# Attention stages in pairs of heads, value and output projection woven in

## The reference

```
stick:  z = q k^T * scale;  log_keep = past ? -softplus(z) : 0
        tail = reversed cumsum(log_keep) - log_keep
        w = past ? exp(log_sigmoid(z) + tail) : 0;   out = (w v) @ w_o
moba:   q, k turned by partial rotary; with 256 tokens there is one block,
        so causal softmax(q k^T * scale) v;           out = (...) @ w_o
mla:    q from a normed latent (head 64 + 32 rotary), k and v from another,
        causal softmax(...) v;                        out = (...) @ w_o
```

## Time and profile before

| | |
|---|---|
| median of 3 runs | 2904.25 us (2901.33 to 2906.99) |
| profiled execution | span 2897.5 us, 44300 instructions; the page gives no other time of it |
| PE busy | 2740.8 us (95%) |
| PE weight loads busy | 2491.1 us (86%) |
| DVE busy | 1697.9 us (59%) |
| ACT busy | 1285.5 us (44%) |
| DMA | 454.85 MB, 157 GB/s over the span |
| chain that ended last | PE 87%, DVE 6%, ACT 4%, issue 1%, DMA 1% |

### The profile page before, as it was taken

The page is one execution under the profiler, slowest core; times in us unless marked ns, Lnnn a source line. Parts: engine busy times, 40 slices in busy tenths (PEclk is TensorE's granted clock), DMA queues, the critical chain, the costliest instruction groups (busy, mean ns, idle before and its releaser), DMA issues.

```text
span 2897.5 us, 44300 instructions
## 1 busy us (share of the span) xinstructions
PE 2740.8 (95%) x18332; PEld 2491.1 (86%) x18342; DVE 1697.9 (59%) x1903; ACT 1285.5 (44%) x1376; POOL 6.8 (0%) x17
## 2 busy tenths in 40 slices
PE   7899998998999989999988999999799999998998
PEld 6689886997999869999976799999679999986997
DVE  6665576656555546565555455655655565564555
ACT  5443454334434544443433434444444444355433
POOL 0000000000000000000000000000000000000000
PEclk9899998999999999999998999999899999998999
DMA  7245432554454325545432255454315545541452
GB/s 270 87 177 189 174 139 82 194 191 148 162 189 165 139 84 184 194 174 187 179 139 80 101 189 189 175 188 170 115 45 201 179 171 201 184 153 70 163 185 73
DMA packets 63473, 454.85 MB, mean 157 GB/s; under 512 B 7104, under 2 KB 7360, under 8 KB 8848
## 3 DMA queue, kind: packets, MB, share of 16 engines
q1 hardware_dynamic: 61920, 448.82, 42.7%
q0 software_dynamic: 1024, 3.51, 0.3%
q10 hardware_dynamic: 432, 1.13, 0.1%
HBM read 452.38 MB, written 1.05 MB: 156 GB/s over the span
## 4 chain that ended last, share of the span: by engine, by line
PE 87%; DVE 6%; ACT 4%; issue 1%; DMA 1%; SPq 0%; DVEq 0%; ACTq 0%
PE tb L226 14%; PE tb L229 14%; PE tb L228 14%; PE acc L257 11%; PE acc L258 10%; PE acc L259 10%; DVE w_lo L206 2%; PE acc L226 1%; PE acc L228 1%; PE acc L229 1%; ACT w_hi L199 1%; PE tb L634 1%; PE tb L288 1%; PE acc L664 1%; PE tb L632 1%
## 5 line engine op out<-in xcount | busy, mean ns | idle before, releaser
L206 DVE TENSOR_TENSOR w_lo<-raw,w_hi 128x2048 fp32r<-128x2048 f32 x426 | 973.8, 2290 | 477.6 <-ACT w_hi L199 477.6
L199 ACT ACTIVATE w_hi<-raw 128x2048 fp32r<-128x2048 f32 x426 | 811.6, 1910 | 582.6 <-PE tb L229 302.9
L226 PE MATMUL tb<-xT,w_hi 128*128 128x256 f32 x3520 | 1004.0, 285 | 15.0 <-DVE w_lo L206 12.4
L228 PE MATMUL tb<-xT,w_hi 128*128 128x256 f32 x3520 | 997.4, 283 | 0.0
L229 PE MATMUL tb<-xT,w_lo 128*128 128x256 f32 x3520 | 997.2, 283 | 0.0
L226 PEld LDWEIGHTS tb<-xT,w_hi 128*128 128x128 f32 x3520 | 676.4, 192 | 24.4 <-DVE w_lo L206 8.1
L228 PEld LDWEIGHTS tb<-xT,w_hi 128*128 128x128 f32 x3520 | 676.6, 192 | 4.5
L229 PEld LDWEIGHTS tb<-xT,w_lo 128*128 128x128 f32 x3520 | 676.6, 192 | 0.0
L257 PE MATMUL acc<-w_hi,cat 128*128 128x512 f32 x1152 | 453.1, 393 | 10.1 <-DVE cat L674 6.5
L258 PE MATMUL acc<-w_hi,cat 128*128 128x512 f32 x1152 | 450.7, 391 | 0.0
L259 PE MATMUL acc<-w_lo,cat 128*128 128x512 f32 x1152 | 449.4, 390 | 0.0
(11 more groups left out here) (260 smaller groups left out, 2427.3 us busy)
## 6 DMA issues: line engine op xcount, KB each, us to landing
raw<-in_stream SPq DMA_DIRECT2D x426, 1024.0 KB, 4.8
h<-in_x SPq DMA_DIRECT2D x2, 512.0 KB, 4.9
gain<-in_gains POOLq DMA_DIRECT2D x2, 512.0 KB, 9.3
xn<-in_gates POOLq DMA_DIRECT2D x2, 512.0 KB, 8.4
out<-xn SPq DMA_DIRECT2D x2, 512.0 KB, 2.7
cst<-in_consts ACTq DMA_DIRECT2D x1, 960.5 KB, 12.5
big<-in_pT POOLq DMA_DIRECT2D x2, 256.0 KB, 3.0
gain<-in_gains POOLq DMA_DIRECT2D x1, 320.0 KB, 3.6
```

The costliest lines, as they stand in the source:

```text
L199: act.activation(w_hi[:, k % SPLIT, :], raw[:, k % RAW, :], ACT.Copy).then_inc(hi_done, 1)
L206: dve.tensor_tensor(w_lo[:, k % SPLIT, :], raw[:, k % RAW, :], w_hi[:, k % SPLIT, :], ALU.subtract).then_inc(lo_done, 1)
L226: pe.matmul(dst(f), hi, src[:, kt, 0, :], start=kt == 0 and (after is None or f == 0), stop=False, skip_group_check=after is not None)
L228: pe.matmul(dst(f), hi, src[:, kt, 1, :], start=False, stop=False, skip_group_check=after is not None)
```

## The change

- `plan` now lists the products of chunks 3 to 11, in the order query, key, value for each group of four heads; the stream is laid out in that order. `begin` makes only the first query, key and value chunk, with the spread of the norm's factor in the middle of the second.
- Value chunks are poured between heads too; ACT takes them (`v_take`).
- Heads go in pairs in moba and mla: the scores of both heads lie in banks 0 and 1 of `tb`, the transposes of both in banks 2 and 3, and each DVE step works on both. The scores of pair p wait for the exponentials of pair p-1; transposes and outputs follow one step behind the scores. In stick the outputs follow one step behind too, instead of two.
- In stick ACT does exponential and logarithm one after the other, after a load of one table set that holds both.
- The output weights are cut into four blocks of 512 rows by 512 columns (`block_chunks`). 18 of the 32 blocks of passes (`OUT_EARLY`) are put into steps 6, 7 and 8, in mla too; the other 14 follow in `out_rest`, which sets the transposes of the next stage before its last four.
- A step has 22 units in stick, 24 in moba and none in mla; its list is cut into three portions beforehand.

```
+        def heads_out(pe, i, m, v, w):
+            g, at = m // 2, SEQ * (m % 2)
...
-            o = acc[p0:p0 + HD, g % 2, at:at + SEQ]
-            pe.matmul(o, v[:, 0, hd * HD:(hd + 1) * HD], w[:, 0:SEQ], start=True, stop=True)
-            pe.matmul(o[:, P:SEQ], v[:, 1, hd * HD:(hd + 1) * HD], w[:, SEQ:CAUSAL], start=False,
-                      stop=True, skip_group_check=True).then_inc(*sig("head_out", (i, hd)))
+            o = [acc[HD * u:HD * u + HD, head_bank(g), at:at + SEQ] for u in range(2)]
+            for u in range(2):
+                hd = 2 * m + u
+                pe.matmul(o[u], v[:, 0, hd * HD:(hd + 1) * HD], w(u)[:, 0:SEQ], start=True, stop=True)
+            for u in range(2):
...
+        OUT_EARLY = ([(0, t, kt) for t in range(2) for kt in range(4)] + [(1, t, kt) for t in range(2) for kt in (4, 5)]
+                     + [(2, 0, kt) for kt in range(4)] + [(3, 0, kt) for kt in (4, 5)])
...
+        def out_rest(pe, i, c, n):
+            pe.wait_ge(*when("cat_lo", (i, 3)))
+            out_block(pe, c, 1, 0, 6)
+            out_block(pe, c, 1, 0, 7).then_inc(*sig("acc_done", (c, 0, 0)))
+            out_block(pe, c, 1, 1, 6)
+            out_block(pe, c, 1, 1, 7).then_inc(chunk_used, 1)
+            out_block(pe, c, 3, 0, 6)
+            out_block(pe, c, 3, 0, 7).then_inc(*sig("acc_done", (c, 0, 1)))
+            for kt in range(4):
+                last = out_block(pe, c, 2, 1, kt)
+            last.then_inc(chunk_used, 1)
+            flip_lower(pe, n)()
+            for kt in range(4, KT):
+                last = out_block(pe, c, 3, 1, kt)
+            last.then_inc(chunk_used, 1)
...
-        def plan(turned, per_step, ahead):
+        FED = 12
+        BLOCKS = [[], [], [], [], [], [], [0, 1, 2, 3], [4, 5, 6, 7], list(range(8, 18))]
...
             seq = []
-            for e in range(2, 8):
...
                 for u in range(UNITS):
-                    if turned and u == 4:
+                    if turned and u == 4 and (e - 1) % 3 != 2:
                         seq.append(("rotate", e - 1))
                     seq.append(("product", e, u))
...
-            return first, [rest[k:k + per_step] for k in range(0, len(rest), per_step)]
-        PLAN = {"moba": plan(True, 9, 5), "stick": plan(False, 18, 0)}
+            steps = []
+            for p in range(HEADS // 2 + 1):
+                units = rest[per_step * p:per_step * (p + 1)] + [("block", k) for k in BLOCKS[p]]
+                n = -(-len(units) // 3)
+                steps.append([units[0:n], units[n:2 * n], units[2 * n:]])
+            return first, steps
+        PLAN = {"moba": plan(True, True, 24, 6), "stick": plan(True, False, 22, 6), "mla": plan(False, False, 1, 0)}
...
+        def fed_bank(e):
+            return acc[:, (2, 0, 1)[e] if e < 3 else (2, 0)[(e - 3) % 2], :]
+        def fed_taken(eng, kind, i, e):
+            if e % 3 == 2:
+                eng.wait_ge(*when("v_out", (i, e // 3)))
+            else:
+                eng.wait_ge(*when("turned" if kind == "moba" else "taken", (i, e)))
...
+            def block(self, k):
+                pe, i, c = self.pe, self.i, self.c_out
+                j, t, kt = OUT_EARLY[k]
+                if k == 0 or OUT_EARLY[k - 1][0] != j:
+                    pe.wait_ge(lo_done, c + j + 1)
+                if (j, kt) == (0, 0) and self.kind != "mla":
+                    fed_taken(pe, self.kind, i, 10 + t)
+                if k in (0, 8):
+                    pe.wait_ge(*when("cat_lo", (i, 1 if k == 0 else 2)))
+                last = out_block(pe, c, j, t, kt)
+                if k == 7:
+                    last.then_inc(chunk_used, 1)
...
+            def begin(self, n):
+                turned = self.kind == "moba"
+                for u in range(UNITS):
+                    self.product(0, u, x_ready(self.pe, n))
+                for u in range(UNITS):
+                    if u == 8:
+                        spread(self.pe, n)
+                    self.product(1, u)
+                self.pe.wait_ge(*when("rb", n))
+                for u in range(UNITS):
+                    if turned and u in (4, 14):
+                        self.rotate(u // 14)
+                    self.product(2, u)
                 self.run(self.first)
...
+            for p in range(N_PAIRS + 1):
+                if p < N_PAIRS:
+                    if p % 2 == 0:
+                        group_ready(p // 2)
+                    if p:
+                        pe.wait_ge(*when("exps", (i, p - 1)))
+                    for u in range(2):
+                        pe.matmul(tb[:, u, 0:P], q(2 * p + u)[:, 0:P], k(2 * p + u)[:, 0:P], start=True, stop=True)
+                    for u in range(2):
+                        pe.matmul(tb[:, u, P:CAUSAL], q(2 * p + u)[:, P:SEQ], k(2 * p + u), start=False, stop=True,
...
+                    last.then_inc(*sig("scores", (i, p)))
+                feed.some(p, 0)
+                if p >= 1:
+                    m = p - 1
                     pe.wait_ge(*when("weights", (i, m)))
-                    if m >= 2:
-                        pe.wait_ge(*when("flip_out", (i, m - 2)))
-                    map_transpose(pe, 2 + m % 2, probs[:, m % 4, :], (i, m))
-                feed.some(2)
-                if s >= 3:
-                    m = s - 3
+                    if m:
+                        pe.wait_ge(*when("flip_out", (i, m - 1)))
+                    for u in range(2):
+                        for j in range(3):
+                            last = pe.transpose(tb[:, 2 + u, j * P:(j + 1) * P],
+                                                probs[:, 2 * (m % 2) + u, j * P:(j + 1) * P], ident)
+                    last.then_inc(*sig("flipped", (i, m)))
+                feed.some(p, 1)
+                if p >= 1:
+                    m = p - 1
                     pe.wait_ge(*when("flip_out", (i, m)))
-                    heads_out(pe, i, m, v, p_T[m % 2])
-                feed.some(1)
-            project_out(pe, i, c_out, n)
...
+        def softmax_act(act, i, scale, p_T, joined, behind):
+            for p in range(N_PAIRS + 1):
+                if p < N_PAIRS:
+                    act.wait_ge(*when("top", (i, p)))
+                    for u in range(2):
...
+                    last.then_inc(*sig("exps", (i, p)))
+                behind(p, 0)
+                if p >= 1:
+                    m = p - 1
                     act.wait_ge(*when("flipped", (i, m)))
-                    if m >= 2:
-                        act.wait_ge(*when("head_out", (i, m - 2)))
-                    act.activation(p_T[m % 2], tb[:, 2 + m % 2, 0:CAUSAL], ACT.Copy).then_inc(*sig("flip_out", (i, m)))
...
+                    if m >= (2 if joined else 1):
+                        act.wait_ge(*when("head_out", (i, m - (2 if joined else 1))))
+                    if joined:
+                        last = act.activation(p_T(m, None), tb[:, 2:4, 0:CAUSAL], ACT.Copy)
+                    else:
+                        for u in range(2):
+                            last = act.activation(p_T(m, u), tb[:, 2 + u, 0:CAUSAL], ACT.Copy)
+                    last.then_inc(*sig("flip_out", (i, m)))
+                behind(p, 1)
+                behind(p, 2)
+                if p >= 2 and p % 2 == 0:
+                    cat_hi(act, i, p // 2 - 1)
...
-                feed.some(3)
-                if 1 <= p <= HEADS // 2:
+                feed.some(p, 0)
+                if p >= 1:
                     m = p - 1
                     pe.wait_ge(*when("keeps", (i, m)))
...
-                feed.some(2)
-                if p >= 2:
-                    m = p - 2
+                feed.some(p, 1)
+                if p >= 1:
+                    m = p - 1
                     pe.wait_ge(*when("sticks", (i, m)))
-                    for u in range(2):
-                        heads_out(pe, i, 2 * m + u, b_v, s_w[m % 2][:, u, :])
-                feed.some(1)
-            project_out(pe, i, c + 12, n)
+                    if m % 2 == 0:
+                        pe.wait_ge(*when("v_out", (i, m // 2)))
+                    heads_out(pe, i, m, b_v, lambda u: s_w[m % 2][:, u, :])
...
+            act.preload_act_table_set("natural_log_exp_and_others")
+            for p in range(N_PAIRS + 1):
+                if p < N_PAIRS:
                     e = s_e[p % 2]
                     act.wait_ge(*when("z_neg", (i, p)))
                     act.activation(e, e, ACT.Exp, scale=scale).then_inc(*sig("own_act", ("e", i, p)))
-                if 1 <= p <= HEADS // 2:
+                    act.wait_ge(*when("own_act", ("e", i, p)))
+                    act.activation(e, e, ACT.Ln, bias=1.0).then_inc(*sig("soft", (i, p)))
+                behind(p, 0)
+                if p >= 1:
                     m = p - 1
                     act.wait_ge(*when("tails", (i, m)))
...
                     act.activation(s_w[m % 2], z_banks(m), ACT.Exp, scale=scale).then_inc(*sig("sticks", (i, m)))
-                if p < HEADS // 2:
```

(57 more changed lines are left out.)

319 lines of the change are left out of this document (174 added, 145 removed).

## The result

The changed kernel takes 2823.74 us (median of 4 runs, 2822.84 to 2824.80), the kernel before on the same chip 2904.09 (2901.33 to 2906.99): ratio 0.9724, 95% interval 0.9713 to 0.9736. Forecast were 2821 us and a range of 2790 to 2858.

The account below looks back on a forecast made before the run. Attention stages were taken as bound by bare pairs and TensorE's waits in them. Gains of 25.1 and 25.4 (stick) and 43 (moba) less 10 (mla) give 83.5 us, from 2904.25 to 2820.75; eight in ten, 2790 to 2858.

Parts of the forecast that it names:

- the wait of the norm factors: Head of a stick stage: TensorE waits 1.2 us, not there before, for the input of the norm factors' spread.
- The stalls of 1 us in the fed steps: Stick steps 0 to 5: late DVE splits delay the weights, stalling TensorE 0.4 us in two steps, 1 us counted.
- that of 2 in step 7: Stick tail: TensorE, there at 13.4 us, waits 2 us for the weights of pair 6, done at 15.4.
- I count nothing for them: Stick pairs: two table loads of 1.283 us a pair leave ACT, 16 a stage; no gain counted beyond the fit.
- case 4: Stick: compiler keeps the table loads, 2.6 us in two fed and three tail steps, twice 13, 2847 us; chance 4%.
- the predicted wait of the outputs in step 6: Moba tail: pair 6's maxima, exponentials and then the copy of pair 5's transposes come late; TensorE waits 5 us.
- the stalls for the turns: Moba steps: product e+2 waits for DVE's turn of e, behind a split and the pair's weights; 4 us in all.
- Mla, a loss of 10 forecast: Mla: both banks hold one pair, outputs wait for ACT's copy behind the next exponentials, clock falls; 79.5 us against 69.6.
- I take 7.8: Mla pairs: 7.8 us each assumed, between 6.7 and 8.9 at 1.2 GHz; six pairs 46.8 us.
- The 6.75 us between span and median: Whole kernel: median 2904.25 us lies 6.75 above the profiled span 2897.5; added to 2814.0 to give 2820.75.
- Case 3: Attention stages: nearly only TensorE's work is left, stick 122, moba 124, mla no loss, 2787 us; chance 10%.
- Cases 2 and 5: Stick and moba pair steps: DVE/ACT orders catch TensorE more, 2855 us, 22%; DVE's pair work late every step, 2910 us, 4%.

## Why the prediction was right, step by step

- **Stick, 127.5 forecast, 127.9 measured, twice.** First scores 22.1 us in (22.2), the wait of the norm factors 0.9 (1.2), the first step 8.96 (9.1), then five of 11.96 (11.9), steps 6 to the end 37.0 (36.7). The stalls of 1 us in the fed steps did not come, that of 2 in step 7 was 0.3. They were closer than the sum shows: I had the weights ready 9.0 us into a step with a late split and TensorE there at 8.7; in the step from 971.55 it was 8.67 and 8.82. Stage by stage the forecast holds because it went through the order of one step on each engine.
- **The joined table, "I count nothing for them".** The forecast time needed no term for it, since the table is there. But the reason that stands with it, that ACT has slack, is wrong, and my own 9.0 against 8.7 spoke against it: there was no room for 2.6 us. So is the price of case 4: 13 us a stage, measured 21.1 and 19.3. Without the table half of the change's gain is gone.
- **Moba, 137 forecast, 133.9 measured.** Head 23.9 (23.9), first step 12.8 with its wait of 2.1 for the take (10.5, and 1.1 of stalls), tail 36.4 (36.5) with the predicted wait of the outputs in step 6, 3.9 us (5). The five steps took 12.0 to 12.9 us (12.4), and the pair's maps 1.06 us where I took 1.3. Mis-sized: the stalls for the turns, 4 us in all, of which 0.7 came beside the first.
- **Mla, a loss of 10 forecast, 13.9 measured.** The mechanism is the one predicted, with its wait of the outputs for ACT's copy and the fallen clock. Mis-sized is the term "I take 7.8" us a pair, between 6.7 at full and 8.9 at half clock: it was 8.5, and the chain by itself 6.4. The granted clock was 0.65 in the steady pairs, with TensorE busy 22.2 of 33.3 us at that clock; I had put it halfway although already had a stretch at 0.57. By the Trainium skill (TensorE: Matmul & The Clock Gate, "HAM oscillation") idle gaps between bursts make the clock fall again and again; this trace agrees, with half clock in 54.6 of the stage's 163.1 us (23.9 before).
- **Sum, 83.5 forecast, 82.1 measured.** The gain was put 3.3 too low in moba, 0.8 too high in stick and 3.9 too high in mla. That these nearly cancel is luck; that every stage went the way forecast, and within 4 us, is not.
- **The 6.75 us between span and median** I carried over as if it were constant. It was not overhead: the time of a run is its span and 1.8 us. Before's profiled execution had a short first block of layers (304.6 us, after 311.9), and so most likely a span below its usual one. Subtracting the gain from the median came out right, for a reason that I had not seen.
- **The rivals.** Case 3 (nearly only TensorE's work is left) holds in stick (1.4 us idle) and almost in moba, not in mla; but its 122 and 124 us lie below TensorE's own work there, 126.5 and 125.8. Cases 2 and 5 price late work of VectorE and ACT; it exists, with margins near zero, and what keeps it from TensorE is the joined table and the 22 units of a step, as the runs without the one or with 13 units show.
- A feed-forward stage stays at 190.4 us (190.0 in the stretch of the earlier trace rows, whose marks are 0.4 us closer).

## What to carry to other kernels

Read an engine's room from the order of one step, start to start, and from the gap between the end of a result and its use, not from its busy sum: here ACT was half idle and had 0.1 us to spare. When a loop is made wider (two heads for one), count the buffers that alternate: if the wider body takes them all, the stages of the loop run one after another, and an order that waits for a copy queued behind the next body's work is the same chain in another place. Waits on TensorE are paid twice where the clock falls in them, so a stage with nothing to weave in wants a deeper pipeline, not a wider body alone.

## What the runs showed that I had not expected

- Products of zeros in a wait, 12 of 512 columns a pair, shortened the kernel by 11.7 us: the granted clock went from 0.65 to 1.00, a pair from 8.5 to 6.43 us.
- Code that no edit touched moved by up to 9 us between profiles (304.6 to 313.5 us for two stages), with the lengths of its stretches at half clock. It is a floor for what one profile's span can tell. A stage at full clock agrees to 0.1 us between profiles (stick 127.9 to 128.0 in all eight that leave it alone). A stage whose clock falls does not: mla in pairs, the same code, took 163.1 us in after and 160.7 to 162.9 in the four other profiles that leave it alone. So its loss of 13.9 is known to some 2 us, and differences of one or two us in such stages are left open.
- In the kernel without the joined table a lower clock in the waits made up 6.0 of the first stage's 21.1 us, beside the waits themselves.
